# An mLSTM layer with carry and local sum in one PSUM group, half of the z gate projected in steps 4 and 5, and the next layer's conditioning computed beside the projections

## The reference

```python
s_qk = einsum('bhctd,bhcsd->bhcts', q, k) * exp(log_d - m_t[..., None])
a_t  = exp(inter - m_t)
num  = (einsum('bhcts,bhcsv->bhctv', s_qk, v)
        + a_t[..., None] * einsum('bhcvk,bhctk->bhctv', c_st, q))
den  = sum(s_qk, -1) + a_t * einsum('bhck,bhctk->bhct', n_st, q)
out  = num / maximum(abs(den), exp(-m_t))[..., None]
...
hh = hsum * sigmoid(o);  hh = rmsnorm(hh, g_head)
y  = (hh * silu(z)) @ w_out                 # o, z, v: h @ w_in, 1024 columns each
x  = x + gt * rmsnorm(y, g_post)            # gt, and the next layer's shift and scale: c @ w_ada + b_ada
```

## Time and profile before

| | us |
|---|---|
| three runs | 1562.94, 1563.14, 1565.64 (median 1563.14) |
| profiled execution, its own time | 1564.55 |
| its span | 1562.7 |
| PE busy | 1469.1 (94%) |
| DVE busy | 993.5 (64%) |
| ACT busy | 754.6 (48%) |
| first product of step 0, of step 6 | 698.50, 783.38 |
| first product on the latent tiles (`l_pTlh`) | 832.77 |

### The profile page before, as it was taken

How to read it: one execution, slowest core, us unless ns; L and a number is a source line. 1 busy time by engine, 2 the same in 40 slices (tenths; PEclk the granted TensorE clock), 3 DMA queues, 4 the chain that set the end, 5 groups by cost and what they waited for, 6 DMA issues and landing times.

```text
span 1562.7 us, 24142 instructions
## 1 busy us (share of the span) xinstructions
PE 1469.1 (94%) x9392; PEld 1204.4 (77%) x9392; DVE 993.5 (64%) x2286; ACT 754.6 (48%) x1630; POOL 67.5 (4%) x76
## 2 busy tenths in 40 slices
PE   6999999999999999999979999897999899999999
PEld 4777766777778777888757777576787798799987
DVE  4647677565566648535684677666777476777763
ACT  4436566453655443331143555555566347455542
POOL 0000000100000100020010100001101020000000
PEclk9999999999999999999989999899999999999999
DMA  9121180222560332221461253333435542445554
GB/s 362 55 108 55 57 316 21 102 82 67 189 230 1 108 102 81 94 68 54 170 221 54 76 159 102 139 98 126 162 125 155 197 161 95 149 148 189 189 189 135
DMA packets 59866, 202.84 MB, mean 130 GB/s; under 512 B 7694, under 2 KB 10984, under 8 KB 59624
## 3 DMA queue, kind: packets, MB, share of 16 engines
q1 hardware_dynamic: 53568, 192.84, 35.5%
q10 hardware_dynamic: 6008, 7.40, 2.1%
q0 software_dynamic: 176, 1.06, 0.2%
HBM read 199.43 MB, written 1.84 MB: 129 GB/s over the span
## 4 chain that ended last, share of the span: by engine, by line
PE 72%; DVE 15%; ACT 5%; DMA 4%; issue 3%; POOL 1%; SPq 0%; ACTq 0%; POOLq 0%; DVEq 0%
PE ps L2243 66%; PE ps L2246 5%; DVE w_l L2913 3%; DVE st L3012 1%; ACT w_h L2556 1%; DVE l_P L2917 1%; DVE x L2921 1%; DMA w_l_ada<-in_l_ada 1%; DMA w_raw<-in_l_out 1%; DVE m_P L3496 1%; ACT l_P L2559 1%; DVE l_xn L2917 1%; DVE l_h_lat L2921 1%; DMA w_raw<-in_l_ada 1%; POOL mstat L3590 1%
## 5 line engine op out<-in xcount | busy, mean ns | idle before, releaser
L2913 DVE TENSOR_TENSOR w_l<-w_raw,w_h 128x1024 fp32r<-128x1024 f32 (+3 forms) x263 | 315.4, 1206 | 74.9 <-ACT w_h L2556 74.4
L2556 ACT ACTIVATE w_h<-w_raw 128x1024 fp32r<-128x1024 f32 (+3 forms) x263 | 272.1, 1042 | 109.6 <-DMA w_raw<-in_f_down 25.3
L2243 PE MATMUL ps<-w_h,l_hTh 128*128 128x512 f32 (+1 forms) x384 | 156.2, 407 | 0.5 <-DVE w_l L2913 0.4
L2243 PE MATMUL ps<-w_h,l_hTl 128*128 128x512 f32 (+1 forms) x384 | 151.8, 395 | 0.0
L2243 PE MATMUL ps<-w_l,l_hTh 128*128 128x512 f32 (+1 forms) x384 | 151.8, 395 | 0.0
L2559 ACT ACTIVATE l_P<-ps,st 128x512 f32<-128x512 f32 (+1 forms) x128 | 77.6, 608 | 91.5 <-DVE st L2921 64.2
L3012 DVE TENSOR_REDUCE st<-ps 128x1 f32<-128x512 f32 (+2 forms) x112 | 72.7, 649 | 43.9 <-PE ps L2243 43.7
L2243 PE MATMUL ps<-f_hTh,w_h 128*128 128x256 f32 x352 | 99.2, 282 | 0.0
L2243 PE MATMUL ps<-f_hTl,w_h 128*128 128x256 f32 x352 | 99.1, 281 | 0.0
L2243 PE MATMUL ps<-f_hTh,w_l 128*128 128x256 f32 x352 | 99.0, 281 | 0.0
L2243 PE MATMUL ps<-l_hTh,w_h 128*128 128x512 f32 (+1 forms) x264 | 97.5, 369 | 0.5 <-issue 0.5
(11 more groups left out here) (444 smaller groups left out, 3467.9 us busy)
## 6 DMA issues: line engine op xcount, KB each, us to landing
w_raw<-in_l_ada SPq DMA_DIRECT2D x49, 512.0 KB, 5.3
w_raw<-in_l_z SPq DMA_DIRECT2D x32, 512.0 KB, 3.5
w_raw<-in_l_adg SPq DMA_DIRECT2D x32, 512.0 KB, 3.9
w_raw<-in_l_out SPq DMA_DIRECT2D x32, 512.0 KB, 4.7
w_raw<-in_m_merge SPq DMA_DIRECT2D x24, 512.0 KB, 3.3
w_raw<-in_f_gate SPq DMA_DIRECT2D x22, 512.0 KB, 3.3
w_raw<-in_f_up SPq DMA_DIRECT2D x22, 512.0 KB, 3.2
w_raw<-in_f_down SPq DMA_DIRECT2D x22, 512.0 KB, 4.2
```

The lines of the kernel that those rows point to most:

```text
L2243: return p.e.matmul(out, lhsT, rhs, start=start, stop=stop)
L2556: return p.e.activation(out, a, func, scale=scale)
L2913: return p.e.tensor_tensor(out, a, b, op)
```

## The change

1. **One PSUM group.** For x = 2..7 the carried state is multiplied with a q that has been scaled by a_t (`qa`), all 257 columns at once, and added to the local product in the same bank. So `two`, `carry`, the DVE operations on them and `ml_edge` go, and h takes one operation per head. New is `ml_scaled`: PE spreads a_t over the partitions (four 128x128 matmuls `ps<-l_arl,l_pick`), DVE writes `qa` (one 128x512 product). The transposes of the a row go. `l_arl` and `l_arc` are made beside the gates by two copies on ACT and two operations on DVE.
2. **z.** `zg(0)` fills steps 0 to 3, `zg(1)` fills steps 4 and 5, context tiles first.
3. **Conditioning.** The blocks (3, 0) go beside q, k and o, the blocks (3, 1) beside `prepare`. Only the gate's eight blocks stay, after step 6.
4. **Finish.** The context pair's finish begins in step 4. Its turns use bank 2 alone. `fin_rows` comes in halves, the latent pair's o gate, squares and rstd tile by tile. Buffers move.

The diff, cut to its core (what moves buffers only is left out):

```diff
@@ layer_mlstm
+        mod = p.ada(TRANS, [(3, 0)])
+        for x in range(8):
             p.dense = ATT
             tiles(qk, 1)
             p.dense = DENSE
             drain(upto(other, 4))
+            if x > 3:
+                drain(upto(mod, 2))
+        drain(mod)
         m.flush()
         f = p.fence()
-        weave(m.prepare(f, ATT), m.og(1, hT, f), 16, 4)
+        weave(along(m.prepare(f, ATT), p.ada(TRANS, [(3, 1)]), 6, 4), m.og(1, hT, f), 16, 4)
...
-        weave(upto(steps, 14), chain(m.zg(0, hT, f), m.zg(1, hT, f)), 28, 14)
+        weave(upto(steps, 14), m.zg(0, hT, f, LAT + CTX), 16, 14)
...
-        gate, ctx = Gate(p, 2, *gate, f), m.finish(CTX, f, (2,))
-        mod = p.ada(PAIR, [(3, 0), (2, "gate"), (3, 1)], gate)
-        drain(braid(upto(steps, 6), upto(mod, 6), upto(ctx, 3)))
-        gate.free = p.fence()
-        drain(braid(steps, mod, ctx))
-        p.W.split_to(len(p.W.order) + 1, len(p.W.order) + 1)
+        ctx = m.finish(CTX, lambda: done, (2,))
+        weave(along(upto(steps, 6), upto(ctx, 4), 4, 6), m.zg(1, hT, f, CTX + LAT), 16, 6)
+        m.flush()
+        done = p.fence()
+        gate, post = p.ends(2, base, 0, len(m.tiles), (97, 105, 125.25, 121.25, 113, 32))
+        mod, lat = p.ada(PAIR, [(2, "gate")], Gate(p, 2, *gate, done)), m.finish((1, 0), lambda: done, TRANS)
+        weave(along(upto(steps, 3), upto(mod, 6), 2, 1), upto(ctx, 5), 5, 3)
+        weave(along(along(steps, mod, 2, 1), ctx, 3, 1), upto(lat, 2), 2, 3)
+        p.W.split_to(len(p.W.order) + 2, len(p.W.order) + 2)
@@ chunks
+            if x < 6:
+                scaled(x + 2)
@@ finish
         for t in pair:
             p.fin_o(self, t, [self.htok[t, h] for h in range(4)])
             yield
-        for t in pair:
             p.fin_sq(self, t)
-            yield
             p.rows_rstd4(self, t)
-        for t in pair:
-            p.fin_rows(self, t)
             yield
         for kp in range(4):
+            for t in pair if kp % 2 == 0 else ():
+                p.fin_rows(self, t, kp)
+                yield
@@ PE
+    def ml_local_mm(p, m, x, d, c, t, bo):
         for h in range(4):
             p.wait_ge(("lstm", "D", x), ("lstm", "ones"), ("lstm", "v", t, h // 2), p.B.freed[bo[h]])
+            y = p.mm(p.n.bank(bo[h], 257), m.Dt[x][:, h * 128:h * 128 + 128], m.va[:, t, h, :], True, c == 0)
+            if c == 0:
+                y.then_inc(*p.mark("lstm", "sum", x, h))
         for h in range(4) if c else ():
-            p.wait_ge(("lstm", "den", x))
-            p.mm(p.n.bank(bo[h])[:, 257:512], m.qk[:, h, t * 128:t * 128 + 128], m.C[:, 4 * d + h, 0:255], True, True).then_inc(
-                *p.mark("lstm", "carry", x, h))
+            p.wait_ge(("lstm", "qa", x), ("lstm", "C", x - 2, h))
+            p.mm(p.n.bank(bo[h], 257), m.qa(x)[:, h], m.C[:, 4 * d + h, :], False, True).then_inc(*p.mark("lstm", "sum", x, h))
+
+    def ml_scaled(p, m, x, d, t, b, out):
+        s0 = slice(t % 2 * 128, t % 2 * 128 + 128)
+        p.wait_ge(("gates", "ar"), p.B.freed[b])
+        for h in range(4):
+            pick = m.pick[:, 4 * d + h:4 * d + h + 1].to_broadcast([128, 128])
+            y = p.mm(p.n.bank(b)[:, h * 128:h * 128 + 128], pick, m.ar[t // 2][:, s0], True, True)
+        y.then_inc(*p.mark("lstm", "spread", x))
@@ DVE
+    def ml_scaled(p, m, x, d, t, b, out):
+        four = p.n.bank(b).rearrange("p (h t) -> p h t", h=4)
+        p.wait_ge(("lstm", "spread", x), ("lstm", "qk", t), ("lstm", "state", x - 4, 3) if x in (4, 5) else None)
+        p.tt(out, m.qk[:, 0:4, t * 128:t * 128 + 128], four, ALU.mult).then_inc(*p.mark("lstm", "qa", x))
```

135 lines of the change are left out of this document (57 added, 78 removed).

## The result

The changed kernel takes 1576.72 us (1573.88 to 1580.66) against 1563.04 for the kernel before beside it: ratio 1.0108, interval 1.0085 to 1.0132, 13.7 us slower. The forecast was 1567.6 and its range ended at 1574. The direction was right, the size was not.

What follows compares the result with a forecast made beforehand. PE was taken to bound the layer up to step 6, one DVE order the tail. 786.9 + 19.5 + 30.6 = 837.0 for the first latent product, against 832.8, gave a median of 1567.6 us; range 1557 to 1574.

Steps and rivals of the forecast that it cites:

- Part 1: Stretch before step 0: sixteen blocks 8.0, turns 0.7, transposes -0.3, a_t operations 0.2; step 0 possible at 700.8.
- the moved DMAs "at nothing": Before step 0: loads of moved raw blocks cost nothing, covered by 5.6 us of PE work on dense blocks.
- the a_t operations at 0.2: Before step 0: four small ACT and DVE operations ahead of a weight split, up to 0.7 us if uncovered, 0.2 taken.
- Part 2: Steps 0 to 5: 84.1 us of work plus 2 of waits, so step 6's local product starts at 786.9.
- +2: Steps 0 to 5: net PE waits, 5.3 us in all with some replacing earlier waits; between 0 and +4.5.
- Part 3: Step 6's local product to DVE's copies of step 7's denominators: 19.5 us (17 to 22.5), against 10.8 before.
- 3.75: Between steps 6 and 7: us from issue to landing of the first output load, taken from the kernel before.
- rival C: Slower still: idle PE halves the clock, last products +3 us and step 7 +1.5; 1572 us, chance 0.14.
- Part 4: DVE's copies of step 7's denominators to the first latent product: 30.6 us (29 to 33), against 38.6 before.
- 13.6 + 4.7: Tail after step 7: DVE chain 13.6 us, then squares, rstd, row pair and the split freeing the fourth product group 4.7.
- A: Faster: output loads land early, tail waits as before and PE runs through; 1558 to 1560 us, chance 0.22.
- B: No change: step waits near nothing with landings as forecast, or waits with early landings; +1, 1564 us, chance 0.28.

Runs made afterwards that it cites:

- two_banks: The changed kernel with the context pair's turns on two PSUM banks in turn, same order; 1572.93 us, ratio 1.0072 against the kernel before.
- acc_cond: The kernel before with only the PSUM group and the moved conditioning; z, finish, banks and splits as before; 1564.09 us, ratio 1.0021.
- acc_cond_row: acc_cond with the gate's eight conditioning blocks in one row behind step 6; 1572.78 us, ratio 1.0081 against the kernel before.
- acc_ar_late: The kernel before with the PSUM group alone and the operations making the a_t rows issued late; 1562.93 us against 1560.61, ratio 1.0013.
- acc_cond_ar: acc_cond with the operations making the a_t rows issued late; 1563.61 us against 1562.21 for the kernel before, ratio 1.0005.

## Why the prediction was right or wrong

**Part 1** (before step 0) failed in size, 13.5 between mark and E where 8.6 was taken, and 1.5 more ahead of the mark that belongs to nothing in the change. The blocks (8.0 taken, 7.6 measured) were right. What failed is the step that cost the moved DMAs "at nothing" and the a_t operations at 0.2. Three things came on top. The a_t operations, bounded at 0.7, made a wait of 1.45. Eight products from 617.5 ran at 0.43 in place of 0.23, 1.5 us at 1.2 GHz (granted clock 0.53 from 617.5 to 621). And PE waited 1.25 at 691.75 for `l_ST`, whose copy on ACT stood behind a split that waited for its load:

```profile
690.15 1.06 ACT L2567 ACTIVATE w_h<-w_raw 128x1024 fp32r<-128x1024 f32 x1 [7.52 <-DMA w_raw<-in_l_o]
691.12 0.58 ACT L2567 ACTIVATE l_ST<-ps 128x512 f32<-128x512 f32 x1
```

The prediction asked whether the moved blocks' own loads arrive; the late one was the load of a dense block that now stands behind them in the ring (before, no split of ACT waits for a load there). These aren't all firm: over the nine profiles with the same order up to E the wait on `l_ST` is between 0 and 1.5, and two_banks has neither it nor the low clock. The distance is 109.1 in two_banks and at most the 111.9 of the changed kernel; with the a_t rows late it is 108.0, 108.5 and 110.3. So the term should have been +10.7 to +13.5, and the profile of the changed kernel shows its upper end.

**Part 2** (E to L) held within 1.5: 87.64 against 86.1. The waits ahead of the local products of steps 1 and 2 are 1.04 each (1.1 to 1.3 taken), step 0's is 1.33 (0.6 taken), a step's four carried products 1.55 to 1.83 (1.8 taken), a spread 0.39 to 0.43 (0.38 taken). The waits sum to 4.9 (5.3 taken), but the kernel before has only 0.5 there, so +2 was too little: the prediction had set off more than 3 against waits that its row of step 4 seemed to hold. Cheaper products made up for part of it. The price of thin filling between z tile and local product was read rightly from the earlier trace rows.

**Part 3** (L to D), 22.6 against 19.5, had the right mechanism in the right place: turn 1 waits 5.13 on ACT `l_fhf` and starts at L + 16.3, step 7 at L + 17.2 (15.5 to 16 taken). ACT and SP of the changed kernel, answering to the earlier trace rows:

```profile
799.98 5.42 SPq L3665 DMA_DIRECT2D w_raw<-in_l_out  x6
```

```profile
806.34 1.06 ACT L2567 ACTIVATE w_h<-w_raw 128x1024 fp32r<-128x1024 f32 x1 [10.79 <-DMA w_raw<-in_l_out]
807.30 0.37 ACT L2567 ACTIVATE gt_rows<-ps 128x256 f32<-128x256 f32 x1
807.70 0.54 ACTq L2606 DMA_DIRECT2D gt_rows<-in_l_b_ada  x1
808.29 2.00 ACT L2567 ACTIVATE w_h<-w_raw 128x1024 fp32r<-128x1024 f32 x2 [0.62 <-ACT gt_rows L2567]
810.20 0.82 ACT L2569 ACTIVATE l_fhf<-ps,l_g 128x256 f32<-128x256 f32 x2
```

Two sizes were off. The first output load took 6.36 from issue (799.98) to split (806.34), not 3.75. The last two gate blocks had been issued 1.0 and 0.5 us ahead of it (799.02 and 799.45), while before the last conditioning block was issued at 791.4 and the output's first at 797.2. The gate's loads in the changed kernel, first and last start:

```profile
L3665 SPq DMA_DIRECT2D w_raw<-in_l_adg x6: 328/328/479, 790.7 to 799.5; - x6
```

So 3.75 was the price of a load with nothing close ahead of it. The first landing was taken at L + 7 and came at L + 11.6. By the Trainium skill (DMA: Bandwidth & Descriptors, "Anatomy of one DMA") 2.0 us plus the bytes at 436 GB/s would be 3.2 us; the page gives this for DMAs that GpSimd issues, and the loads here are issued by SP, which the prediction didn't say. The trace doesn't agree for a load that was issued right behind others. And step 7's first products took 3.40 (811.98 to 815.38) instead of 1.8, half clock behind 5 idle us, which had been put into rival C and not into the sum.

**Part 4** (D to T), 33.7 against 30.6. The DVE chain up to the split that frees the fourth group of products was read right: it was taken as 13.6 + 4.7 = 18.3, and the first of the two splits below (834.82 plus half of 2.35) ends at 836.0, 18.7 behind D.

```profile
817.32 0.35 DVE L2939 COPY l_dn<-ps 128x1 f32<-128x1 f32 x4 [5.11 <-PE ps L2255]
...
834.82 2.35 DVE L2928 TENSOR_TENSOR w_l<-w_raw,w_h 128x1024 fp32r<-128x1024 f32 x2
```

(The wait at 836.14 is put down to ACT `w_h`, which had ended before; it was this `w_l`.) Behind it 14.84 for 30 products and four turns where 12.3 was taken, with a wait of 2.14 on `l_h_lat` and two stretches at 0.43 per product. The prediction had the chain and named the clock as a rival of its own, though the earlier trace rows have 0.66 to 0.82 in three windows of this stretch. The Trainium skill (TensorE: Matmul & The Clock Gate, "HAM oscillation") says that idling between bursts returns the clock to half; the trace agrees with granted clocks of 0.73 to 0.83 from 800 to 850, but acc_cond ran its step 7 at full clock behind 2.96 idle.

**The steps that failed** in the sum are thus three: the moved loads and operations ahead of step 0, put at 0.2 where 2.7 of waits came (and 1.5 of low clock); the price of an output load, 3.75 where 6.36 was measured; and the clock behind idle stretches, left out of the sum, where step 7's local products took 3.40 instead of 1.8 and the closing products and turns 14.84 instead of 12.3.

**What was never asked** is a matter of frame, not of a term. The prediction took L to T as one DVE chain, of which the change removes a few links, and compared it with the kernel before only. Its own rows spoke against a chain without holes: in the window with the least PE (6.19, from 800 to 810) DVE stands at 6.94, not above 9. It never asked what the tail would be with the lighter work in the old order. acc_cond and its two relatives answer: 38.6 to 42.7 with almost the same instructions, where the changed kernel takes 56.2. By the single edits, the row of eight blocks with its late loads (7.4 to 11.5 of L to T in acc_cond_row), turn 1 behind a copy that stands behind three splits (4.4 by two_banks), step 7 behind the turns (2.8) and the late split (3.8) make the difference. They overlap and don't add up exactly.

The parts may depend on each other. The group alone is worth 0.0%, the moved blocks alone cost 0.48%, and both together 0.21%, or 0.05% with the a_t rows late. From L to T both give 6.7 to 10.8 and one alone 1.1 or 3.6, which fits a tail that PE's blocks and DVE's h operations limit in turn. The intervals of these ratios overlap, so this is read from the distances and not shown by the times.

**Rivals.** A (faster) needed the output's block 2 on chip before L + 9; even block 0's split began at L + 11.6. B (no change) needed small waits in the steps and early landings, and got neither. C (the clock) happened where it had been put (step 7's 1.6, and a dozen of the last products at 0.43) and in Part 1 besides (1.5). Forecast plus C is 1572, still some 5 short, and that is about Part 1's two waits (2.7) and the load that took 2.6 longer than its price.

## What to carry to other kernels

When a change takes work from a stage that two engines limit in turn, cost the changed stage in the old order first: an order is a decision of its own, and here it was worth 13.5 to 17.6 us of the tail, more than the edits themselves gave. Blocks that read a fixed ring of buffers belong two by two between other work, not more in a row than the ring holds (0.6% in the plain order); in the changed order that alone gave only 0.27%, since the next wait took its place. And count, for each moved load, the load that now stands behind it, and put the low clock into the sum, as a range, wherever the sum has an idle stretch ahead of products. Last, read a stage's length from more than one profile before explaining a few us of it: here one order gave tails 4.1 us apart.

## What the hardware showed that was not expected

- A load of 512 KB took 3.75 us from issue to use where the load ahead of it had been issued 5.8 us earlier, and 6.36 right behind two others, with the window at 360 GB/s.
- In the changed kernel's profile eight products from 617.5 to 620.5 ran at 0.43 (1.2 GHz) with PE busy throughout since the wait of 1.45 that ended 15 us before. Ten kernels show such a stretch between mark and E, acc_ar_late and acc_eight among them, which have no PE wait from the mark up to there. In two_banks, with the same instructions up to there and the same wait (at 601.20), the products ran at 0.23. The order alone doesn't decide it; the cause is open.
- The same instructions behind the same idle time ran at either clock: step 7's four local products took 1.74 us in acc_cond and 3.42 in acc_cond_ar, each behind a wait of 2.96.
- A product that follows conditioning blocks takes 0.34 until the next starts (637.26 to 637.60) in place of 0.23.

```profile
635.39 1.93 PE L2255 MATMUL ps<-w_raw,cT 128*32 128x256 f32 x32
637.26 0.50 PE L2255 MATMUL ps<-l_hTh,w_h 128*128 128x512 f32 x1
637.60 0.39 PE L2255 MATMUL ps<-l_hTl,w_h 128*128 128x512 f32 x1
```

  Over the five groups in which the sixteen blocks stand that is about half a microsecond, which the price by the blocks' own duration leaves out. (Part of it follows any break: behind the wait at 602.53 the next product starts after 0.31.)
